# Twelve gather slots and two weight places instead of eleven and three, with one token tile's first four heads searched late in the third stage

## The reference, cut to what matters

```python
def peer(h, wq, subkeys, u_tab, v_tab):
    q = (t @ wq).reshape(-1, PEER_HEADS, 2, PEER_QDIM // 2)          # 8 heads
    s = jnp.einsum('thpd,hpkd->thpk', q, subkeys)                    # 2 x 128 scores a head
    sv, si = lax.top_k(s, PEER_TOPK)                                 # 16 of 128, twice
    cv, ci = lax.top_k(<sums of the two lists>, PEER_TOPK)           # 16 of 256
    idx = i1 * PEER_KEYS + i2
    g = jax.nn.softmax(cv, axis=-1)
    act = gelu(einsum('td,thkd->thk', tb, u_tab[ib]))
    out = einsum('thk,thkd->td', (gb * act), v_tab[ib])              # 128 rows of u and v a token
```

## Time and profile before

| | us |
|---|---|
| median of 3 runs | 2312.08 (2311.71 to 2313.92) |
| the profiled execution's own time | 2313.23 |
| its span, first to last instruction | 2311.4 |
| TensorE busy | 2062.1 (89%) |
| VectorE busy | 1598.1 (69%) |
| moved by DMA | 939.55 MB, mean 406 GB/s |

### The profile page before, as it was taken

The page is one execution under the profiler, slowest core; times in us unless marked ns, Lnnn a source line. Parts: engine busy times, 40 slices in busy tenths (PEclk is TensorE's granted clock), DMA queues, the critical chain, the costliest instruction groups (busy, mean ns, idle before and its releaser), DMA issues.

```text
span 2311.4 us, 23775 instructions
## 1 busy us (share of the span) xinstructions
PE 2062.1 (89%) x6896; PEld 1117.8 (48%) x6896; DVE 1598.1 (69%) x3904; ACT 952.3 (41%) x2791; POOL 1009.6 (44%) x868
## 2 busy tenths in 40 slices
PE   8998999999998888988999998898799987787787
PEld 7785554555564434443555554346456532222222
DVE  3865778967766668888866668755766887766454
ACT  2024444543334444444454334534543544444333
POOL 0003445344434544445445445420333555566763
PEclk9999999999999999999999999999899999999999
DMA  9979999999999999999999999986799999999997
GB/s 405 425 293 387 426 426 427 427 426 427 426 426 427 427 427 424 426 426 427 415 427 426 428 426 427 424 314 256 296 378 404 418 426 427 427 427 427 427 427 327
DMA packets 132610, 939.55 MB, mean 406 GB/s; under 512 B 14720, under 2 KB 17920, under 8 KB 18944
## 3 DMA queue, kind: packets, MB, share of 16 engines
q0 software_dynamic: 110592, 805.36, 83.2%
q1 hardware_dynamic: 21888, 132.68, 13.8%
HBM read 936.93 MB, written 1.05 MB: 406 GB/s over the span
## 4 chain that ended last, share of the span: by engine, by line
PE 39%; DMA 30%; DVE 14%; issue 6%; POOL 6%; ACT 4%; SPq 0%; another core or an unknown queue 0%; POOLq 0%; DVEq 0%; ACTq 0%
DMA uv<-uv_dram,stage_idx 28%; PE psum L998 21%; PE psum L801 10%; POOL uv L1071 6%; DVE uv L1600 5%; PE psum L783 4%; PE psum L941 1%; DVE h L1302 1%; DMA uv<-in_dram 1%; DMA uv<-ada_dram 1%; ACT diag L1245 1%; PE psum L716 1%; PE psum L972 1%; ACT small L1241 1%; DVE si L1543 0%
## 5 line engine op out<-in xcount | busy, mean ns | idle before, releaser
L998 PE MATMUL psum<-uv,diag 128*128 128x512 f32 x3072 | 1437.9, 609 | 199.4 <-ACT diag L1245 188.8
L1071 POOL DMA_INDIRECT uv<-uv_dram,stage_idx x768 | 974.4, 1269 | 993.1 <-PE psum L998 729.3
L1600 DVE CUSTOM_DVE_ANT_0 uv<-uv,h 128x1024 f32<-128x1024 f32 x768 | 932.9, 1225 | 509.9 <-DMA uv<-uv_dram,stage_idx 484.7
L998 PEld LDWEIGHTS psum<-uv,diag 128*128 128x128 f32 x3072 | 561.9, 192 | 970.4 <-issue 519.0
L1239 ACT ACTIVATE small<-small 128x1 f32<-128x1 f32 x768 | 155.0, 202 | 989.6 <-DVE small L1600 988.2
L1245 ACT ACTIVATE diag<-const,small 128x128 f32<-128x128 f32 x768 | 308.5, 402 | 25.2
L801 PE MATMUL psum<-hT,wring 128*128 128x256 f32 (+1 forms) x1312 | 273.5, 362 | 0.7 <-ACT hT L1109 0.7
L801 PEld LDWEIGHTS psum<-hT,wring 128*128 128x128 f32 x1312 | 233.5, 191 | 60.2 <-issue 33.0
L1241 ACT ACTIVATE small<-small,gw 128x1 f32<-128x1 f32 x768 | 226.2, 295 | 24.9
L1057 POOL COPY stage_idx<-idx 128x8 uint32<-128x8 uint32 x96 | 35.0, 365 | 278.6 <-DVE idx L1571 278.0
L1091 ACT ACTIVATE work<-psum 128x256 f32<-128x256 f32 (+2 forms) x123 | 48.0, 391 | 151.8 <-PE psum L801 114.6
(11 more groups left out here) (220 smaller groups left out, 1285.9 us busy)
## 6 DMA issues: line engine op xcount, KB each, us to landing
uv<-ada_dram SPq DMA_DIRECT2D x28, 1024.0 KB, 18.1
wring<-wq_dram SPq DMA_DIRECT2D x24, 1024.0 KB
wring<-in_dram SPq DMA_DIRECT2D x23, 1024.0 KB
uv<-uv_dram,stage_idx POOLq DMA_INDIRECT x768
uv<-in_dram SPq DMA_DIRECT2D x11, 1024.0 KB, 23.5
uv<-ada_t_dram SPq DMA_DIRECT2D x10, 1024.0 KB, 25.8
wring<-ada_dram SPq DMA_DIRECT2D x8, 1024.0 KB
uv<-out_w_dram SPq DMA_DIRECT2D x4, 1024.0 KB, 21.1
```

Of the source, the lines that this page charges most:

```text
L998: last = mm(acc[:, b, :], diag[:, s % DIAGS, :], uv[:, s % RING, D + 512 * b:D + 512 * (b + 1)], start=(c == 0), stop=(c == NSEL - 1))
L1071: nc.gpsimd.indirect_dma_start(out=uv[:, r, :], out_offset=None, in_=tables[stage // 2], in_offset=bass.IndirectOffsetOnAxis(ap=places[:, ...
L1600: v.tensor_tensor_reduce(out=uv[:, r, 0:D], in0=uv[:, r, 0:D], in1=h2[:, row_of[stage], t, :], scale=1.0, scalar=0.0, op0=ALU.mult, op1=AL ...
```

## The change

Four things change together.

1. `RING` goes from 11 to 12 and `WRING` from 3 to 2: the gather of slot s now waits for the values of slot s - 12, and weight block n of the ring for the last use of block n - 2 instead of n - 3. `ss_heads` and `ms_heads` share one tile. `LAST_SLOTS` moves by one.
2. `heads_by_tile`, now used in stage 0 alone, takes tile 1's query and score of head 1 right behind those of head 0, so that both early blocks are given back before head 2's is fetched; its four stretches start and end up to three slots later.
3. In the third stage `heads_apart` replaces it. Heads 2 and 3 are queried, scored and searched for tile 0 alone, at slots 14 to 23 and 18 to 34 of the stage (17 to 26 and 26 to 36 before). Tile 1's norm and transpose move from slots 12 to 17 to slots 22 to 32. Tile 1's query, score and search of heads 0 to 3 stand at slots 112 + 22h to 132 + 22h. The search of head 1 in `early` moves from slots 3 to 10 to slots 1 to 7.
4. Late queries need their weights and keys again: `reloaded` holds for heads 0 to 3 of the third stage, three `wq` blocks and four `keys` more than before. Keys are counted by load (`key_loads`) instead of by head.

```diff
-WRING = 3
+WRING = 2
...
-LAST_SLOTS = (5, 6, 7, 8, 9, 10)
+LAST_SLOTS = (6, 7, 8, 9, 10, 11)
...
-RING = 11
+RING = 12
...
+def heads_apart(stage):
+
+    one, two = (0,), (1,)
+    out = [(14, 17, query(stage, 2, one) + score(stage, 2, one)), (17, 23, find(stage, 2, one)),
+           (18, 23, query(stage, 3, one) + score(stage, 3, one)), (24, 34, find(stage, 3, one)),
+           (22, 32, rms(stage, two) + norm(stage, 1)[1:] + [("turn_back", stage, 1)]),
+           (33, 39.5, query(stage, 4) + score(stage, 4) + query(stage, 5))]
+    for h in range(KEPT):
+        out.append((112 + 22 * h, 132 + 22 * h, query(stage, h, two) + score(stage, h, two) + find(stage, h, two)))
+    return out
...
-             (5, 7, [("o_norm", 2, 1, 0, HEADS)]), (7, 8, [("o_turn", 2, 1, 0, HEADS)]), (3, 10, find(2, 1, one)),
-             (10, 12, out_t[1])]
+             (6, 8, [("o_norm", 2, 1, 0, HEADS)]), (8, 9, [("o_turn", 2, 1, 0, HEADS)]), (1, 7, find(2, 1, one)),
+             (9, 13, out_t[1])]
...
-    return stage == 2 and h == 1
+    return stage == 2 and h < KEPT
...
-                pe.wait_ge(keys_landed[h % 2], 16 * (stage * PH // 2 + h // 2 + 1))
+                pe.wait_ge(keys_landed[load % 2], 16 * (load // 2 + 1))
```

More of the change, by code:

```diff
@@ L168, in heads_by_tile @@
     one, two = (0,), (1,)
-    return [(first, first + 5, rms(stage, two) + norm(stage, 1)[1:] + [("turn_back", stage, 1)] + query(stage, 0, two)
-             + score(stage, 0, two)),
-            (first + 5, first + 14, query(stage, 2) + score(stage, 2, one) + find(stage, 2, one) + score(stage, 2, two)),
-            (first + 14, first + 24, query(stage, 1, two) + score(stage, 1, two) + query(stage, 3) + score(stage, 3, one) + find(stage, 3, one)
-             + score(stage, 3, two)),
-            (first + 24, 39, query(stage, 4) + score(stage, 4) + query(stage, 5))]
+    return [(first, first + 8, rms(stage, two) + norm(stage, 1)[1:] + [("turn_back", stage, 1)] + query(stage, 0, two)
+             + score(stage, 0, two) + query(stage, 1, two) + score(stage, 1, two)),
+            (first + 8, first + 16, query(stage, 2) + score(stage, 2, one) + find(stage, 2, one) + score(stage, 2, two)),
+            (first + 16, first + 26, query(stage, 3) + score(stage, 3, one) + find(stage, 3, one) + score(stage, 3, two)),
+            (first + 26, 39, query(stage, 4) + score(stage, 4) + query(stage, 5))]
+def heads_apart(stage):
[7 more added lines that the diff above has]
+    return out
 def kept_heads(stage):
@@ L264, in schedule @@
             own = early if stage else [(0, 2, find(0, 1, one)[3:]), (0, 2, out_rows(0, 1))]
-            for first, last, steps in own + heads_by_tile(stage, 12 if stage else 8) + kept_heads(stage):
+            for first, last, steps in own + (heads_apart(stage) if stage else heads_by_tile(stage, 8) + kept_heads(stage)):
                 placed += spread(steps, at + first, at + last)
@@ L344, in weight_blocks, with keys_of @@
     return list(blocks.values())
+def keys_of(stage, h, tiles):
+    return stage, h, tiles if reloaded(stage, h) else 0
 def reloaded(stage, h):
-    return stage == 2 and h == 1
+    return stage == 2 and h < KEPT
 def weight_places(program, blocks):
@@ L409, in build @@
         unused = small[:, 30 + 3 * RING:38 + 3 * RING]
-        ss_heads, ms_heads = (sb(s, [P, 16]) for s in ("ss_heads", "ms_heads"))
-        root_heads = ms_heads
+        ss_heads = ms_heads = root_heads = sb("ss_heads", [P, 16])
         smax, nmax, psums = (sb(s, [P, 2, 2]) for s in ("smax", "nmax", "psums"))
@@ L596, in build @@
         scored = {}
+        key_loads = list(dict.fromkeys(keys_of(*item[1:]) for kind, item in program if kind == "step" and item[0] == "score"))
         block = ctx.enter_context(nc.Block())
@@ L965, in score @@
                 k = stage * PH + h + 1
+                load = key_loads.index(keys_of(stage, h, tiles))
                 pe.wait_ge(act_took, n["qh", stage, h])
-                pe.wait_ge(keys_landed[h % 2], 16 * (stage * PH // 2 + h // 2 + 1))
+                pe.wait_ge(keys_landed[load % 2], 16 * (load // 2 + 1))
                 bank = to_act.open(pe)
@@ L971, in score @@
                         o = (q * len(tiles) + i) * P
-                        last = mm(bank[:, o:o + P], qh[:, h % 2, q, t * P:(t + 1) * P], keys[:, h % 2, q * PK:(q + 1) * PK],
+                        last = mm(bank[:, o:o + P], qh[:, h % 2, q, t * P:(t + 1) * P], keys[:, load % 2, q * PK:(q + 1) * PK],
                                   start=True, stop=True)
                 to_act.fill(last)
-                if tiles[-1] == TT - 1:
-                    scored[k] = (act_bank_full, to_act.n)
+                scored[load] = (act_bank_full, to_act.n)
                 for t in tiles:
@@ L1009, in _ @@
             sp.dma_start(const[:, 0:W_EARLY], A["const"][:, 0:W_EARLY]).then_inc(const_loaded, 16)
-            heads = 0
+            load = 0
             for n, (kind, layer, b, _, _) in enumerate(blocks):
@@ L1032, in _ @@
                 sp.dma_start(w_home(n), A[kind][layer, b]).then_inc(w_landed[w_slot[n]], 16)
-                if kind == "wq" and b == heads % PH:
-                    heads += 1
-                    if heads > 2:
-                        sp.wait_ge(*scored[heads - 2])
-                    sp.dma_start(keys[:, b % 2, :], A["keys"][layer, b]).then_inc(keys_landed[b % 2], 16)
+                if kind == "wq":
+                    assert key_loads[load][1] == b
+                    if load >= 2:
+                        sp.wait_ge(*scored[load - 2])
+                    sp.dma_start(keys[:, load % 2, :], A["keys"][layer, b]).then_inc(keys_landed[load % 2], 16)
+                    load += 1
             for t in range(TT):
```

2 lines of the change are left out of this document (1 added, 1 removed).

## The result

The changed kernel takes **2341.58 us** (median of 4 runs, 2340.50 to 2345.16), the kernel before 2311.99 us in the same comparison. The ratio is 1.0132, its 95% interval 1.0120 to 1.0144: 29.6 us slower. The prediction was 2303.2 us with a range of 2299 to 2311, so it was wrong in sign and in size. The profiled execution of after has a span of 2338.7 us.

The account below looks back on a forecast made before the run. The prediction took the time as bytes at 427 GB/s plus DMA idle time. 8.6 - 15.2 - 1.2 - 2.3 + 1.2 = -8.9 us from 2312.1 gave 2303.2 us, range 2299 to 2311.

Parts of the forecast that it names:

- the slowest, at 2318: Rival: in the third stage head 2's weight block lands late and TensorE stands at the query; around 2318 us, chance 0.08.
- Part 1: Three `wq` blocks and four `keys` more, 3.67 MB, fetched from about slot 561 on with no idle to hide in: +8.6 us.
- Part 2: Third stage's start: head 1's indices come at least 7 us earlier, at 1664 or before, closing the first DMA dip.
- The sign that I gave: GpSimd copies head 1's and head 2's indices without a wait of several microseconds before them, the second near 1705.
- Part 3: Third stage: head 2's score at 1692.9, 16 us earlier, indices by 1707, 8 to 12 us ahead of need; second dip closes.
- Part 4: Third stage: 16 us of TensorE work leave the first 50 slots, closing dip three; late heads cost nothing; three dips together -15.2 us.
- The sign was wrong again: Sign for the third stage: TensorE no longer busy 40 of 40 us around 1800.
- The rival of the clock: Rival: with less early work TensorE's clock falls to 1.2 GHz, some 5 us for seven slots; 2308 us, chance 0.03.
- Part 5: Two weight places: a block takes 8.4 us beside gathers, less than every tight place allows; 0 on the sum.
- Part 6: Twelfth place elsewhere: -1.2 us in 1098 to 1156, gap 2.3 us earlier, +1.2 us at the third stage's first gathers, opening 0.
- The opening, which I set at 0: First stage issues seven gathers instead of six before waiting for output weights, but head 2's block comes later: 0.
- The gap: Before the third stage: starts 2.3 us earlier (0 to -3.3); slot 514 waits for the last block's place, +1.2 us (0 to 2.5).

Follow-up runs that it names:

- E1: The changed kernel with 32 unused bytes a partition ahead of `uv`, which then starts at 85248: 2304.96 us, ratio to before 0.9961.
- E7: The changed kernel's order with the kernel before's eleven row places and three weight places, `uv` at 93440: 2311.94 us, ratio to before 0.9988.
- E2: The changed kernel with `psums` allocated behind `uv`, which moves 32 bytes down to 85184: 2337.13 us, ratio to before 1.0105.
- E3: The kernel before with `psums` allocated behind `uv`, which moves 32 bytes down to 93408: 2347.86 us, ratio to before 1.0151.
- E4: The kernel before with `prec` allocated behind `uv`, which moves 64 bytes down to 93376: 2341.10 us, ratio to before 1.0124.
- E11: E6 plus, of the new order, only the list of the attention's tail and head 1's search: 2304.00 us, ratio to before 0.9952.
- E6: The changed kernel, `uv` at 85248, with the third stage in the kernel before's order, heads 0 and 1 fetched twice: 2306.60 us, ratio to before 0.9960.
- E8: The changed kernel, `uv` at 85248, with only heads 0 and 1 of tile 1 late: 2300.68 us, ratio to before 0.9941.
- E12: E8 run once more, unchanged: 2300.10 us, ratio to before 0.9936.
- E5: The kernel before with `nmax`, `psums` and `prec` allocated behind `uv`, which moves 128 bytes down to 93312: 2342.75 us, ratio to before 1.0116.
- E9: The kernel before with five small tiles allocated behind `uv`, which moves 256 bytes down to 93184: 2314.68 us, ratio to before 0.9999.

## Why the prediction was wrong, step by step

**"This kernel's time is its bytes at 427 GB/s plus the time in which DMA has nothing to do."** The step that failed. The sum itself holds within 2 us: with `uv` on a multiple of 256 it gives E1, forecast 2303.2, measured 2304.96. That it is so close is partly luck, since two of its terms missed by 3 and 4 us and cancelled (below). What failed is the constant. I read 427 off and took it as the chip's, when it was also the layout's. Each percent of it weighs 22 us, more than any term that I worked out, and I gave it no bound, no rival and no chance. None of the rivals named a rate; the slowest, at 2318, was still 24 us short. The hint was in the edit itself: `small` holds three numbers for each place, `ms_heads` goes, `wring` shrinks, and all three are allocated ahead of the ring that carries 805 of 943 MB.

**Part 1, bytes, +8.6.** Right: 943.22 MB on the page, 3.67 more.

**Part 2, head 1's indices by 1664.** Right. GpSimd's copies in E1, for heads 1 and 2, which answer to the earlier trace rows:

```profile
1655.92 0.19 POOL L1075 COPY stage_idx<-idx 128x8 uint32<-128x8 uint32 x1 [4.70 <-DVE idx L1589]
...
1702.82 0.19 POOL L1075 COPY stage_idx<-idx 128x8 uint32<-128x8 uint32 x1 [3.17 <-DVE idx L1589]
```

The sign that I gave, copies without a wait of several microseconds, was too strict. GpSimd still waits 4.70 us, but with up to twelve gathers in flight, and DMA runs at 425. The wait of an issuing engine is not idle time of DMA; it is only so from the point where the backlog is gone.

**Part 3, head 2.** Forecast: score at 1692.9, indices by 1707. TensorE in E1, which answers to the earlier trace rows:

```profile
1664.45 3.60 PE L958 MATMUL psum<-wring,work 128*128 128x512 f32 x8
...
1679.90 1.95 PE L818 MATMUL psum<-hT,wring 128*128 128x128 f32 x16
...
1683.41 1.95 PE L818 MATMUL psum<-hT,wring 128*128 128x128 f32 x16
...
1686.91 0.61 PE L990 MATMUL psum<-keys,work 128*128 128x128 f32 x4
```

Right, and 6 us earlier than forecast: the output product moved from 1676.73 to 1671.32 by what part 2 gained, which I had mentioned and not counted. The indices are written at 1702.48.

**Part 4, TensorE's debt and the late heads.** Right in sum: the stretch 1740 to 1820 is at 426, and 1900 to 2270 at 427, beside four late queries. The sign was wrong again: TensorE is still busy 79.29 of 80 us in E1, and 40.00 of 40 in 1780 to 1820 of the changed kernel. Full work and a hole in DMA are two things. It isn't the twelfth place alone that parts them: E7, with eleven, has TensorE busy 80.00 of 80 in the same stretch and DMA at 426. The three holes: 16.1 to 0.5, forecast 16.1 to 0.9. The rival of the clock didn't come: 1900 to 2290 has a granted clock of 0.98 in E1. But my "only the gap's long waits cost it" was a wrong reading: the earlier trace rows have 0.97 in 1098 to 1156, with TensorE busy 54.70 of 58 us.

**Part 5, two places for weights, 0.** Right. After the opening, TensorE's list of waits has one line with a weight block in it:

```profile
PE psum L732 <- DMA wring<-ada_dram: 0.9, 1, 0.9
```

That is the gap's first block, 1.1 us before and 0.5 in E1. In the changed kernel, whose packets are the slower ones, the median from issue to landing of a `wq` block is 9.2 us with twelve gathers in flight, against the 8.4 of the one block of the earlier trace rows; twelve gathers served first would have made it 29.

**Part 6, elsewhere.** 1098 to 1156: forecast -1.2, in E1 415 became 427, **-1.6**. The opening, which I set at 0: 0 to 200 went from 370 to 376 GB/s, **-2.8**, a term that I missed. I weighed one transfer against one, and didn't see that the seventh gather goes out while DMA is otherwise at 144 GB/s. The gap: forecast -2.3 + 1.2 = -1.1, measured **+2.9** (1400 to 1650, 339 to 334 GB/s):

```profile
1400.00:1650.00 250.00, 214.95 (x869) 118.00 (x867) 168.88 (x359) 113.33 (x311) 80.65 (x73) 0.97 0.81 334
```

Its first block was issued at 1547.54 instead of 1553.04, 5.5 us earlier, of which 4.4 is what the opening and 1098 to 1156 had won, so some 1.1 of the forecast 2.3. (The last gather of the second stage was issued at 1533.59 instead of 1539.75, 6.2 us earlier, and the block followed it by nearly as much. So the landing moved with the issue; the end of my range at which it would not have moved didn't come.) The first gather behind the gap came only 1.75 us earlier, at 1626.23, so 3.75 us went inside the gap. TensorE bounds it, and one row of E1 tells most of it; the same window before had a granted clock of 1.00:

```profile
1590.00:1600.00 10.00, 8.37 (x24) 4.65 (x23) 3.49 (x11) 2.43 (x8) 0.00 (x0) 0.66 0.00 2
```

The clock was at 1.2 GHz for part of these 10 us, right behind a pause of TensorE (2.48 of 5 us busy in 1585 to 1590; before the same pause, 2.09 of 5, was followed by 1.00). By 0.66 against 1.00 that is an estimated 3.4 us. E2 and E3 have such a dip at this place, the changed kernel and E4 have not; with the start and the places of E1, E11 has it, and E6, E8 and E12 have not. There is one profiled execution of each, and those of E1 and E11 were the slowest of their five (2305.68 and 2306.78 us). So it may come and go between executions of one kernel, and I don't count it to the change; what tips it is not shown.

**The sum.** 8.6 - 15.6 - 1.6 - 2.8 + 2.9 = -8.5 us for E1 against before, forecast -8.9; the spans differ by 7.5. The two misses of 3 and 4 us cancelled. And +36.6 us for the 32 bytes by which the changed kernel's ring starts too low.

## What to carry to other kernels

Where DMA is saturated, the rate is a term of the sum and not a constant: before an edit that resizes, merges or drops any tile, compare the start addresses of what the transfers write, and keep the largest target of DMA on a multiple of 256 bytes, for instance by allocating it ahead of the small tiles (a place that was not tried here). When a change comes out slower everywhere at once, from its first microseconds on and with the engines as full as before, look for something common to all its instructions, such as a layout, and not at the instructions that it moved. And price each part of an edit in bytes against the hole that it closes: two of this one's four late heads cost more than they brought.

## What the runs showed of the hardware that I had not expected

- The start of a ring within the SBUF partition changes the saturated DMA rate: 427 GB/s from a multiple of 256 bytes, 421 from 128 or 192 past one, 420 from 224 past one; 8192-byte packets of 309 ns became 312 or 313 in the median and 319 to 321 at the 95th percentile, while the engines' share stays at 1.01.
- The slower rows slow their neighbours: `wring` did not move in E3 to E5, yet its packets between slow gathers took a median of 312 or 313 ns instead of 309. A misplaced `wring` among well-placed gathers cost nothing that could be measured.
- It needs no gathers. In the opening the hardware queue alone fills `uv`. The window 20 to 120 of the changed kernel, then of E1, with the same blocks:

```profile
DMA packets 5975, 41.85 MB, mean 418 GB/s; under 512 B 666, under 2 KB 666, under 8 KB 1178
```

```profile
DMA packets 6077, 42.57 MB, mean 426 GB/s; under 512 B 680, under 2 KB 680, under 8 KB 1192
```

  The kernel before and E9 have 426 and 425 there, E2 to E5 have 419 or 420.
